# A block-diagonal query made by transposed copies, and state loads moved to the sync engine, in a two-branch transformer kernel

## The chip, the core and the metric

The kernel runs on one core of a Trainium2 chip. A core has a matrix engine (PE, with its weight loads shown as PEld), a vector engine (DVE), a scalar engine (ACT), GpSimd (POOL) and a sync engine (SP). SP, ACT and POOL can start transfers between the core's memory (SBUF) and the chip's memory; matrix products land in PSUM, which DVE and ACT read. The metric is the device time of one execution in microseconds (us).

## The reference

Two inputs go through the same two-layer network: a prompt of 1024 tokens with no past, and eight running sequences of 16 tokens each, with a past. Layer A mixes tokens with an mLSTM recurrence, layer B with attention; each is followed by a feed-forward block. The change lies in layer A's recurrence alone. Cut to what matters:

```
# c: state [heads=8, 128 values, 64 keys], n: normaliser [8, 64], per sequence
def mlstm_chunk(state, q, k, v, log_gates):          # one chunk of tokens
    weights  = exp(gate_a[key] + gate_b[query])      # masked, causal
    num      = (q k^T * weights) v + decay_q * (q c^T)
    den      = row sums of the same, with n for c
    h        = num / max(|den|, floor)
    c_new    = decay * c + (w k)^T v
    n_new    = decay * n + sum(w k)
    return c_new, n_new, h
```

For the prompt the state starts at zero and is carried through eight chunks of 128 tokens. The eight running sequences together are one tile of 128 rows, 16 rows each, and each has an old state of its own: `state_c` is 8 x 8 x 128 x 64 floats (2 MB), `state_n` 8 x 8 x 64.

## The kernel before

Stages follow one another with a barrier of all engines between them. In A1 the first projection is made. In A2 `mlstm` is run twice: for the prompt (tag `mprompt`) and then for the running sequences (`mrun`). A3 holds layer A's output projection, its feed-forward block and layer B's projections, B1 attention, B2 the rest. Each engine carries out its own instructions in the order in which they are written, and a wait on a semaphore holds all that stands behind it on that engine. There is no planner: the order is the order of the code.

**The prompt.** Each chunk has four units, one for a pair of heads. `turn` (L1365) transposes the next chunk's query, key and weighted query on PE, one part in each of units 1 to 3; ACT copies them out of PSUM (L1474). `scores` (L1376) makes the products of key and query, DVE's `argument` (L1544) and ACT's `exponent` (L1469) the weights, DVE's `weighted_scores` (L1553) their product. `numerator` (L1403, L1411) and the state's increment (L1419) follow on PE, and DVE updates the state (L1587). ACT copies the numerators out (L1504). SP loads each chunk's `qk`, `bb` and `v1` (L1265, L1269, L1273) into one of two slots: for the third chunk on, `qk` waits for `k8_done` two chunks back, `bb` for the arguments, `v1` for the numerators. At the end of the first chunk ACT issues the loads of the old running states, 13 transfers (`load_running_states`, L1476 to L1483): four of `nload`, one of `nold`, and eight of `cold`, 256 KB each in runs of 256 bytes.

**The running tile.** PE first transposes the old states, head by head, through one PSUM bank `pt` (L1345); ACT copies each into `c0t` (L1463), and the next head waits for that copy. Then it transposes query and key (L1365). For the old states' part of the numerator, every row of the tile may meet only its own sequence's state. DVE spreads a head's weighted query over all eight sequences and multiplies by a 0/1 matrix (`masked_q`, L1537), PE transposes the result (L1394) into the same bank, ACT copies it (L1500), and PE multiplies by the turned state (L1399). This is done for each of the eight heads, inside `numerator`. At the end DVE makes the output (L1558 to L1563), decays and adds the normaliser (L1606, L1608), and for each head decays the old state (L1612) and adds PE's increment (L1615, from L1456, whose right side `km` POOL makes at L1335). SP stores each head's state (L1286).

The wait that binds the state turns to one another, and the one in front of each query turn:

```
if h: pe.wait_ge(c0_copied, h)                 # L1343: the one bank is free again
pe.wait_ge(qm_done, h + 1)                     # L1390: DVE's masked query
if h >= 1: pe.wait_ge(qm_copied, h)            # L1392: the one bank again
pe.wait_ge(qm_copied, h + 1)                   # L1397: the turned query
```

Of the kernel before, what the change touches and what calls it, by code (L numbers as in the profile page):

```python
# [11 lines left out]
P = 128  # L12
# [7 lines left out]
CB = 512  # L20
# [1171 lines left out]
def mlstm(nc, g, qkvo, b_d, h_d, running, c_out, n_out, state_c=None, state_n=None):  # L1192
    tag = "mrun" if running else "mprompt"
    N_C = 1 if running else NP
    V1 = A_V + 1
    NPAIR = DEC_BATCH // 2
    with Scope(nc, tag) as s:
        SLOTS = 1 if running else 2
        qk, v1 = s.sb("qk", [P, SLOTS, 2 * A_H * A_QK]), s.sb("v1", [P, SLOTS, A_H, V1])
        qg, k8, wsv = s.sb("qg", [P, SLOTS, A_H * A_QK]), s.sb("k8", [P, SLOTS, A_H * A_QK]), s.sb("wsv", [P, SLOTS, A_H, V1])  # L1200
        qt, kt, qgt = (s.sb(n, [P, SLOTS, A_PAIRS, P]) for n in ("qt", "kt", "qgt"))
        tokc, gcc = s.sb("tokc", [P, SLOTS, 4, A_H]), s.sb("gcc", [P, SLOTS, A_PAIRS])
        arg, st = s.sb("arg", [P, A_PAIRS, 2, P]), s.sb("st", [P, 2, 2, P])
        num = s.sb("num", [P, SLOTS, A_H, V1])
        den, hout = s.sb("den", [P, A_H]), s.sb("hout", [P, A_H, A_V])
        bb = s.sb("bb", [P, SLOTS, A_H, P])
        names = ("ones", "tok_done", "qg_done", "k8_done", "wsv_done", "turned", "t_copied",
                 "arg_done", "exp_done", "score_ready", "st_done", "num_ready", "num_done",
                 "state_ready", "state_done", "h_done", "stored", "chain")
        (ones, tok_done, qg_done, k8_done, wsv_done, turned, t_copied,  # L1210
         arg_done, exp_done, score_ready, st_done, num_ready, num_done,
         state_ready, state_done, h_done, stored, chain_sem) = (s.sem(n) for n in names)
        qk_loaded, v_loaded, b_loaded = ([s.sem(f"{n}{i}") for i in range(SLOTS)] for n in ("qk_loaded", "v_loaded", "b_loaded"))

        psc, pn = s.ps("scores", [P, 2, CB]), s.ps("num_p", [P, 2, CB])
        pc, pt = s.ps("state", [P, CB]), s.ps("turn", [P, 4, P])
        final_t, final_c, final_s, made = (s.sem(n) for n in ("final_t", "final_c", "final_s", "made"))
        LINKS = 4
        PARTS = 2 if running else 3
        if running:  # L1220
            cold, nload, nold, c0t = g.cold, g.nload, g.nold, s.sb("c0t", [P, NPAIR, A_H, V1])
            c_loaded, n_loaded = g.c_loaded, g.n_loaded
            qm, km = s.sb("qm", [P, 2, DEC_BATCH, A_QK]), s.sb("km", [P, 2, DEC_BATCH, A_QK])
            qmt, wsk, ccur = s.sb("qmt", [P, 2, NPAIR, P]), s.sb("wsk", [P, A_H, A_QK]), s.sb("ccur", [P, 2, DEC_BATCH, A_QK])
            c0_turned, c0_copied, qm_done, qm_turned, qm_copied = (s.sem(n) for n in (
                "c0_turned", "c0_copied", "qm_done", "qm_turned", "qm_copied"))
            decayed, km_done, wsk_done, c_ready, c_done, n_ready, n_done = (s.sem(n) for n in (
                "decayed", "km_done", "wsk_done", "c_ready", "c_done", "n_ready", "n_done"))
            mask = g.mask_dec
        else:  # L1230
            ct = s.sb("ct", [P, A_PAIRS, V1])
            cfin, nfin = s.sb("cfin", [P, A_PAIRS, P]), s.sb("nfin", [A_PAIRS, P])
            mask = g.mask_kq

        def tile(i):
            return NT - 1 if running else i

        def chunks(engine, body, chain=None):

            if running:  # L1240
                body(0, 0)
            else:
                run(engine, N_C // SLOTS, lambda i: [body(SLOTS * i + slot, slot) for slot in range(SLOTS)],
                    chain, peel_last=True, per=SLOTS * LINKS)
# [4 lines left out]
        def ahead(i, slot, j, n):  # L1249

            return (i, slot, j + n) if j + n < A_PAIRS else (i + 1, 1 - slot, j + n - A_PAIRS)

        def loads(i, slot):

            return (i - slot) * 8 + 16 if SLOTS == 2 else 16

        with nc.Block() as block:

            @block.sync
            def _(sp):  # L1260
                def load(i, slot):
# [6 lines left out]
                    cols = b_d[:, bass.ds(i * P, P)].rearrange("(o h) n -> o h n", o=1)  # L1268
# [4 lines left out]
                    sp.dma_start(v1[:, slot, :, 0:A_V], qkvo[t, :, A_V0:A_O0].rearrange("t (h v) -> t h v", v=A_V)).then_inc(v_loaded[slot], 16)  # L1273

                chunks(sp, load)
                if not running:
                    wait(sp, final_c, 5)
                    for j in range(A_PAIRS):
                        sp.dma_start(c_out[0, 0, 2 * j:2 * j + 2].rearrange("h v d -> v h d"),
                                     cfin[:, j, :].rearrange("v (h d) -> v h d", h=2)).then_inc(final_s, 16)  # L1280
# [335 lines left out]

# [975 lines left out]
```

## Time and profile before

| | us |
|---|---|
| median of three runs | 3476.12 (3471.89 to 3477.49) |
| the profiled execution | 3474.42 |
| its span, first to last instruction | 3472.9 |
| stages ahead of the recurrence | 0 to 348.50 |
| prompt recurrence | 348.50 to 507.95 (159.45; mean granted PE clock 0.61) |
| running recurrence | 507.95 to 572.87 (64.92; mean granted PE clock 0.76) |
| the rest | 572.87 to the end (PE busy 891.90 of 927.13 up to 1500, 1832.13 of 1972.90 after) |

Over the whole span PE is busy for 92%, DVE for 35%, POOL for 34% and ACT for 17%. The granted clock is the share of PE's full speed that it was given: 0.50 is 1.2 GHz, 1.00 is 2.4 GHz. A busy share is an average over the whole kernel; in the two recurrence stages PE waits for short chains of other engines, and these stages have to be read by themselves.

### The profile page before, as it was taken

The page shows a single profiled execution, that of the slowest core. Times are in us where ns is not written, and L with a number is a line of the kernel's source. Part 1 is how long each engine was busy: PE and PEld are TensorE (multiplying, and loading weights), DVE is VectorE, ACT ScalarE, POOL GpSimd, SP SyncE. Part 2 cuts the span into 40 slices and gives each one's busy share as a digit, 9 for nine tenths or more (in the row PEclk, how much of TensorE's full clock was granted, in tenths as well). Part 3 has the DMA queues.
Part 4 walks back from the last instruction along what each step waited for, and adds up shares of the span by engine and source line. Part 5 has one row for each costly group of instructions (what it writes and reads, how often), then busy time and mean ns, then how long its engine had stood idle before and what let it go on. Part 6 is the DMA issues. An engine that isn't in the chain of part 4 may idle for free. (4 is left out here: it accounts for less than half of the span.)

```text
span 3472.9 us, 43103 instructions
## 1 busy us (share of the span) xinstructions
PE 3205.3 (92%) x17102; PEld 2753.7 (79%) x17102; DVE 1220.6 (35%) x1957; ACT 601.7 (17%) x1211; POOL 1196.8 (34%) x682
## 2 busy tenths in 40 slices
PE   7999674999999999989999959997699999999999
PEld 6787453799999999977888846665479999999998
DVE  3110345633332323346235055542344333322323
ACT  3111222220000000012121124443212000000000
POOL 4330214623233433223242136661152322333320
PEclk9999657999999999999999969999899999999999
DMA  4321633311111111111222142326541111111111
GB/s 137 102 86 49 137 104 115 122 37 37 36 36 48 49 48 36 42 38 63 83 91 83 61 108 74 82 61 247 192 163 37 37 36 36 36 60 48 37 36 55
DMA packets 186788, 259.18 MB, mean 75 GB/s; under 512 B 34292, under 2 KB 124248, under 8 KB 186664
## 3 DMA queue, kind: packets, MB, share of 16 engines
q1 hardware_dynamic: 146072, 187.94, 17.8%
q10 hardware_dynamic: 38672, 64.27, 5.3%
q0 software_dynamic: 1920, 5.24, 0.4%
q8 instruction: 86, 1.41, 0.2%
q14 instruction: 38, 0.31, 0.0%
HBM read 198.95 MB, written 50.48 MB: 72 GB/s over the span
## 5 line engine op out<-in xcount | busy, mean ns | idle before, releaser
L858 PE MATMUL A_bank<-A_xth,A_w 128*128 128x384 f32 x1056 | 353.0, 334 | 0.0
L858 PE MATMUL B_bank<-B_xth,B_w 128*128 128x384 f32 x1056 | 353.0, 334 | 0.0
L860 PE MATMUL B_bank<-B_xtl,B_w 128*128 128x384 f32 x1056 | 352.9, 334 | 0.0
L860 PE MATMUL A_bank<-A_xtl,A_w 128*128 128x384 f32 x1056 | 352.9, 334 | 0.0
L859 PE MATMUL A_bank<-A_xth,A_w 128*128 128x384 f32 x1056 | 352.8, 334 | 0.0
L859 PE MATMUL B_bank<-B_xth,B_w 128*128 128x384 f32 x1056 | 352.8, 334 | 0.0
L61 POOL TENSOR_TENSOR A_w1h<-A_raw_a,g_one 128x1024 fp32r<-128x1024 f32 (+1 forms) x43 | 103.0, 2395 | 552.6 <-PE A_bank L886 323.4
L642 PE MATMUL A_bank<-A_w1h,A_xth 128*128 128x512 f32 x576 | 225.4, 391 | 0.0
L644 PE MATMUL A_bank<-A_w1h,A_xtl 128*128 128x512 f32 x576 | 224.3, 389 | 0.0
L643 PE MATMUL A_bank<-A_w1l,A_xth 128*128 128x512 f32 x576 | 224.1, 389 | 0.0
L958 DVE TENSOR_TENSOR g_x<-B_bank,g_x 128x512 f32<-128x512 f32 x198 | 137.0, 692 | 211.3 <-PE B_bank L886 211.3
L958 DVE TENSOR_TENSOR g_x<-A_bank,g_x 128x512 f32<-128x512 f32 x198 | 136.2, 691 | 202.1 <-PE A_bank L886 202.1
L858 PEld LDWEIGHTS A_bank<-A_xth,A_w 128*128 128x128 f32 x1056 | 198.3, 188 | 0.6 <-issue 0.2
L858 PEld LDWEIGHTS B_bank<-B_xth,B_w 128*128 128x128 f32 x1056 | 198.2, 188 | 0.6 <-issue 0.2
L859 PEld LDWEIGHTS A_bank<-A_xth,A_w 128*128 128x128 f32 x1056 | 198.3, 188 | 0.4
L859 PEld LDWEIGHTS B_bank<-B_xth,B_w 128*128 128x128 f32 x1056 | 198.2, 188 | 0.4
L860 PEld LDWEIGHTS A_bank<-A_xtl,A_w 128*128 128x128 f32 x1056 | 198.3, 188 | 0.0
L860 PEld LDWEIGHTS B_bank<-B_xtl,B_w 128*128 128x128 f32 x1056 | 198.2, 188 | 0.0
L1889 POOL TENSOR_TENSOR fprompt_acc<-fprompt_acc,fprompt_prob 128x512 f32<-128x512 f32 (+3 forms) x160 | 152.6, 954 | 60.2 <-ACT fprompt_prob L2075 44.1
L61 POOL TENSOR_TENSOR B_w1h<-B_raw_a,g_one 128x2048 fp32r<-128x2048 f32 (+1 forms) x15 | 47.2, 3148 | 360.6 <-PE B_bank L886 323.4
L884 PE MATMUL A_bank<-A_w1h,A_w1l 128*128 128x512 f32 x396 | 156.8, 396 | 12.1 <-issue 7.3
L61 POOL TENSOR_TENSOR A_w<-A_raw_a,g_one 128x1024 fp32r<-128x1024 f32 x42 | 85.4, 2032 | 238.1 <-PE A_bank L860 64.4
(444 smaller groups left out, 6603.6 us busy)
## 6 DMA issues: line engine op xcount, KB each, us to landing
frun_v<-in_cache_v_dram SPq DMA_DIRECT2D x8, 2048.0 KB, 8.9
qkvo<-A_wide ACTq DMA_DIRECT2D x54, 256.0 KB, 2.0
A_raw_a<-in_w_in_a_dram SPq DMA_DIRECT2D x24, 512.0 KB, 3.7
A_raw_b<-in_w_gu_dram SPq DMA_DIRECT2D x11, 1024.0 KB
A_raw_a<-in_w_down_dram SPq DMA_DIRECT2D x11, 1024.0 KB, 4.9
B_raw_b<-in_w_gu_dram SPq DMA_DIRECT2D x11, 1024.0 KB
B_raw_a<-in_w_down_dram SPq DMA_DIRECT2D x11, 1024.0 KB, 4.9
A_raw_a<-in_w_gu_dram SPq DMA_DIRECT2D x10, 1024.0 KB
```

The lines of the kernel that those rows point to most:

```text
L61: return pool.tensor_tensor(out, in_, ones, ALU.mult)
L642: pe.matmul(bank[:, :], self.mem.xth[:, k, xs], self.wh[par][:, k], start=(k == 0), stop=False)
L643: pe.matmul(bank[:, :], self.mem.xth[:, k, xs], self.wl[par][:, k], start=False, stop=False)
L644: ins = pe.matmul(bank[:, :], self.mem.xtl[:, k, xs], self.wh[par][:, k], start=False, stop=(k == KC - 1))
L858: pe.matmul(banks[j][:, :], h[:, f, k], xth[:, k, self.thirds[j]], start=(k == 0), stop=False)
L859: pe.matmul(banks[j][:, :], l[:, f, k], xth[:, k, self.thirds[j]], start=False, stop=False)
L860: ins = pe.matmul(banks[j][:, :], h[:, f, k], xtl[:, k, self.thirds[j]], start=False, stop=(k == KC - 1))
L884: pe.matmul(self.yp[c][:, :], self.hh[:, f, ts], self.dh[:, f, cs], start=(f == 0), stop=False)
L958: dve.tensor_tensor(xs, self.yp[c][:, :], xs, ALU.add).then_inc(self.added, 1)
L1889: pool.tensor_tensor(to, to, new, ALU.add).then_inc(summed, 1)
```

## The change

`mlstm` becomes two functions. `mlstm_prompt` is the prompt's branch as it was, but for the loads of the old running states: SP issues them, right behind its loads of the second chunk.

```diff
 def load(i, slot):                               # on SP, in mlstm_prompt
     ...
     sp.dma_start(v1[:, slot, :, 0:A_V], ...).then_inc(v_loaded[slot], 16)
+    if isinstance(i, int) and i == 1:
+        load_running_states()
+def load_running_states():                       # on SP
+    for h in range(A_H):
+        sp.dma_start(g.cold[:, h], ...).then_inc(g.c_loaded, 16)
+    for j in range(NPAIR):
+        sp.dma_start(g.nload[j * A_H:(j + 1) * A_H, :], ...).then_inc(g.n_loaded, 16)
+    sp.dma_start(g.nold[:, :], ...).then_inc(g.nold_loaded, 16)
-        if j == A_PAIRS - 1 and not running and below(i, 1):    # on ACT
-            load_running_states()
```

`mlstm_running` is written anew for the one tile. Its core is below. Between the lines shown, POOL makes `k8`, `wsv`, `wsk` and `km` as before; PE transposes `nload` and makes `scores(1)`; DVE waits for the turned query and the zeroes before `place_q`, which runs four times, makes `weighted_scores(0)` before the decays, and after the weights it decays the normaliser, makes the output and adds the normaliser's sum. ACT copies the three turned parts, takes `exponent(0)` and `exponent(1)`, copies the eight turned states and the normaliser's part, takes the last two exponents and copies the numerators. SP loads `qk`, `bb` and `v1`, and stores the output, the normaliser and each head's state as they are done.

```diff
+STEP = P + 2 * DEC_SEQ
+qm = s.sb("qm", [P, A_H, NPAIR * STEP])          # all eight heads at once
+pt = [s.ps(f"turn{i}", [P, 4, P]) for i in range(2)]      # two banks for turns
+pool.memset(v1[:, :, A_V:V1], 1.0).then_inc(ones, 1)
+pool.memset(qm[:, :, :], 0.0).then_inc(zeroed, 1)
+pool.wait_ge(qk_loaded, 16)
+pool.tensor_tensor(qg, qk[:, 0:A_K0], spread(tok[:, KIND_G, :], A_QK), ALU.mult).then_inc(qg_done, 1)
...
+pe.wait_ge(qk_loaded, 16)
+turn(0, qk[:, 0:A_K0]); turn(1, qk[:, A_K0:A_V0])
+pe.wait_ge(qg_done, 1)
+turn(2, qg)                                      # n >= 2 waits for t_copied n - 1
+pe.wait_ge(t_copied, 2)
+scores(0)
+pe.wait_ge(g.c_loaded, 16 * A_H)
+for h in range(A_H):
+    turn_state(h)                                # bank (h + 1) % 2, h >= 2 waits for c0_copied h - 1
...
+pe.wait_ge(qm_done, 4)
+pe.wait_ge(c0_copied, A_H + 1)
+for j in range(A_PAIRS):
+    numerator(j)
+    if j + 2 < A_PAIRS: scores(j + 2)
+def numerator(j):
+    ...
+    for e in range(2):
+        h = 2 * j + e
+        pe.matmul(pn[:, e, 0:V1], st[:, j % 2, e, :], v1[:, h, :], start=True, stop=False)
+        for n in range(NPAIR):
+            ins = pe.matmul(pn[:, e, 0:V1], qm[:, h, n * P:(n + 1) * P], c0t[:, n, h, :], start=False, stop=(n == NPAIR - 1))
+def place_q(e, half):                            # four copies of 64 x 256, into the zeroed buffer
+    rows = slice(half * A_QK, (half + 1) * A_QK)
+    to = qm[rows, :, :].rearrange("p (j e) (n w) -> p j e n w", e=2, w=STEP)[:, :, e, :, half * DEC_SEQ:(half + 1) * DEC_SEQ]
+    got = qgt[e * A_QK:(e + 1) * A_QK, :, :].rearrange("p j (n s t) -> p j n s t", s=2, t=DEC_SEQ)[:, :, :, half, :]
+    dve.tensor_copy(to, got).then_inc(qm_done, 1)
+def decay(h):
+    dve.wait_ge(c0_turned, h + 1)
+    dve.tensor_tensor(cold[:, h], cold[:, h], spread(g.gc_dec[:, h, :], A_QK), ALU.mult).then_inc(decayed, 1)
+for j in range(A_PAIRS): argument(j)
...
+for h in range(A_H): decay(h)
+for j in range(1, A_PAIRS): weighted_scores(j)
...
+for h in range(A_H):
+    dve.wait_ge(c_ready, h + 1)
+    dve.tensor_tensor(cv, late_bank(h), cv, ALU.add).then_inc(c_done, 1)
```

On PE, at the start of the running tile, the order before is this (`mrun_turn` is the one bank for turns, `A_cold` the old states, `mrun_qm` the masked query):

```order
L1345 MATMUL mrun_turn<-g_ident,A_cold 128x128 x32
L1349 MATMUL mrun_turn<-g_ident,A_nload 128x32
L1365 MATMUL mrun_turn<-g_ident,mrun_qk 128x128 x8
L1376 MATMUL mrun_scores<-mrun_qt,mrun_kt 128x128 x4
L1394 MATMUL mrun_turn<-g_ident,mrun_qm 128x128 x4
L1396 MATMUL mrun_num_p<-mrun_v,mrun_st 128x129
L1399 MATMUL mrun_num_p<-mrun_c0t,mrun_qmt 128x129 x4
```

And this is the order now, on the same engine at the same place:

```order
L1545 MATMUL mrun_turn<-g_ident,mrun_qk 128x128 x8
L1545 MATMUL mrun_turn<-g_ident,mrun_qg 128x128 x4
L1562 MATMUL mrun_scores<-mrun_qt,mrun_kt 128x128 x2
L1554 MATMUL mrun_turn<-g_ident,A_cold 128x128 x32
L1588 MATMUL mrun_turn<-g_ident,A_nload 128x32
L1562 MATMUL mrun_scores<-mrun_qt,mrun_kt 128x128 x2
L1571 MATMUL mrun_num_p<-mrun_v,mrun_st 128x129
L1573 MATMUL mrun_num_p<-mrun_c0t,mrun_qm 128x129 x4
```

The turns of query and key have moved ahead of those of the states, the weighted query is turned once (four transposes), and the 32 transposes of the masked query are gone from between the numerators.

On DVE, the end of the running tile before (from the output's last step to the first head's state):

```order
L1560 RECIPROCAL mrun_den<-mrun_den 128x8
L1563 TENSOR_TENSOR mrun_hout<-mrun_num,mrun_den 128x1024
L1606 TENSOR_TENSOR A_nold<-A_nold,A_gc_s 8x512
L1608 TENSOR_TENSOR A_nold<-mrun_state,A_nold 8x512
L1612 TENSOR_TENSOR A_cold<-A_cold,A_gc_dec 128x512
L1615 TENSOR_TENSOR A_cold<-mrun_turn,A_cold 128x512
```

And DVE's running tile now, from its first instruction to the first head's state:

```order
L1642 SCALAR_TENSOR_TENSOR mrun_arg<-mrun_bb,A_tok,A_mask_dec 128x128 x8
L1657 COPY mrun_qm<-mrun_qgt 64x4x4x16 x4
L1650 TENSOR_TENSOR mrun_st<-mrun_scores,mrun_arg 128x256
L1661 TENSOR_TENSOR A_cold<-A_cold,A_gc_dec 128x512 x8
L1650 TENSOR_TENSOR mrun_st<-mrun_scores,mrun_arg 128x256 x3
L1678 TENSOR_TENSOR A_nold<-A_nold,A_gc_s 8x512
...
L1683 TENSOR_TENSOR mrun_hout<-mrun_num,mrun_den 128x1024
L1685 TENSOR_TENSOR A_nold<-mrun_state,A_nold 8x512
L1690 TENSOR_TENSOR A_cold<-mrun_turn,A_cold 128x512
```

All eight decays, and the normaliser's, have moved from the end to the time of the turns; eight masked queries have become four copies.

On SP, in the prompt, this is the order now, from the second chunk's loads to the third chunk's (which were next to one another before):

```order
L1250 DMA mprompt_qk<-qkvo 128x1024
L1254 DMA mprompt_bb<-mlstm_cum_prompt 128x8x128
L1257 DMA mprompt_v<-qkvo 128x8x128
L1240 DMA A_cold<-in_state_c_dram 128x8x64 x8
L1242 DMA A_nload<-in_state_n_dram 8x2x64 x4
L1244 DMA A_nold<-in_state_n_dram 8x512
L95 UNCONDITIONAL_BRANCH
L48 ISA
L1250 ISA
L1250 DMA mprompt_qk<-qkvo 128x1024
```

The third chunk's `qk`, and all that SP loads after it, now stands behind the 13 transfers.

## Rows read from the trace of the kernel before

**Rows 1.** Timeline of ACT at 377 us: start, duration, engine, line, [idle before <- releaser]
```profile
378.97 15.12 ACTq L1483 DMA_DIRECT2D A_cold<-in_state_c_dram  x8
394.14 0.42 ACT L1469 ACTIVATE mprompt_arg<-mprompt_arg 128x256 f32<-128x256 f32 x1 [16.74 <-issue]
```

**Rows 2.** Timeline of PE, 378 to 396 us
```profile
379.12 0.66 PE L1365 MATMUL mprompt_turn<-g_ident,mprompt_qk 128*128 128x128 f32 x4
...
394.97 1.20 PE L1403 MATMUL mprompt_num_p<-mprompt_v,mprompt_st 128*128 128x129 f32 x4 [14.77 <-ACT mprompt_num L1504]
```

**Rows 3.** Timeline of SP in the prompt recurrence
```profile
355.92 3.29 SPq L1273 DMA_DIRECT2D mprompt_v<-qkvo  x1
...
437.51 0.37 SPq L1273 DMA_DIRECT2D mprompt_v<-qkvo  x1
...
453.48 0.37 SPq L1273 DMA_DIRECT2D mprompt_v<-qkvo  x1
...
465.99 0.37 SPq L1273 DMA_DIRECT2D mprompt_v<-qkvo  x1
```

**Rows 4.** The tile `A_cold`: its loads' issue (ns min/median/max), and issue to landing
```profile
L1483 ACTq DMA_DIRECT2D A_cold<-in_state_c_dram x8: 404/1098/5032, 379.0 to 393.2; - x8
...
DMA to landing us min/median/max: 4.5/7.0/10.7
```

**Rows 5.** The tile `mprompt_qk`: issue to landing of its eight loads
```profile
DMA to landing us min/median/max: 3.7/5.8/11.9
```

**Rows 6.** Timeline of PE in the running recurrence
```profile
509.85 1.09 PE L1345 MATMUL mrun_turn<-g_ident,A_cold 128*128 128x128 f32 x4 [0.78 <-ACT mrun_c0t L1463]
511.72 1.09 PE L1345 MATMUL mrun_turn<-g_ident,A_cold 128*128 128x128 f32 x4 [0.78 <-ACT mrun_c0t L1463]
...
523.46 1.12 PE L1365 MATMUL mrun_turn<-g_ident,mrun_qk 128*128 128x128 f32 x4 [0.32 <-ACT mrun_c0t L1465]
...
552.39 1.02 PE L1446 MATMUL mrun_state<-mrun_wsk,A_own 128*8 128x512 f32 x2
```

**Rows 7.** Timeline of POOL in the running recurrence
```profile
511.74 1.04 POOL L1306 TENSOR_TENSOR mrun_qg<-mrun_qk,mrun_tokc 128x512 f32<-128x512 f32 x1 [3.69 <-DMA mrun_qk<-qkvo]
...
560.57 5.39 POOL L1335 TENSOR_TENSOR mrun_km<-mrun_k,A_own 128x512 f32<-128x512 f32 x4 [0.67 <-PE mrun_turn L1456]
```

**Rows 8.** Groups by line, POOL: the largest memset (busy us, mean ns, idle before)
```profile
L1896 POOL MEMSET fprompt_qx<- 128x4096 f32 x1 | 3.7, 3657 | 0.0
```

**Rows 9.** Timeline of ACT at 527 us
```profile
526.98 0.71 ACT L1469 ACTIVATE mrun_arg<-mrun_arg 128x256 f32<-128x256 f32 x2
```

**Rows 10.** Timeline of PE's weight loads, 530 to 537 us
```profile
531.15 1.79 PEld L1399 LDWEIGHTS mrun_num_p<-mrun_c0t,mrun_qmt 128*128 128x128 f32 x8 [0.56 <-ACT mrun_qmt L1500]
...
534.52 0.97 PEld L1399 LDWEIGHTS mrun_num_p<-mrun_c0t,mrun_qmt 128*128 128x128 f32 x8 [0.65 <-ACT mrun_qmt L1500]
...
536.44 0.42 PEld L1394 LDWEIGHTS mrun_turn<-g_ident,mrun_qm 128*128 128x128 f32 x4 [0.53 <-issue]
```

**Rows 11.** Windows: us, busy (instructions) by engine, granted clock, DMA share, GB/s
```profile
508.00:533.00 25.00, 16.13 (x63) 11.43 (x64) 5.48 (x12) 7.84 (x15) 7.43 (x7) 0.50 0.20 64
534.00:552.00 18.00, 13.10 (x99) 11.16 (x99) 4.71 (x9) 5.52 (x11) 0.00 (x0) 1.00 0.00 1
...
565.00:569.00 4.00, 1.80 (x4) 0.30 (x2) 3.45 (x6) 0.00 (x0) 0.96 (x1) 1.00 0.86 178
```

**Rows 12.** Timeline of DVE at 430 us, in the prompt
```profile
430.70 2.46 DVE L1544 SCALAR_TENSOR_TENSOR mprompt_arg<-mprompt_bb,mprompt_tokc,g_mask_kq 128x128 f32<-128x128 f32 x2
...
433.93 0.61 DVE L1544 SCALAR_TENSOR_TENSOR mprompt_arg<-mprompt_bb,mprompt_tokc,g_mask_kq 128x128 f32<-128x128 f32 x2
```

**Rows 13.** Groups by line, DVE, 507 to 573 us
```profile
L1612 DVE TENSOR_TENSOR A_cold<-A_cold,A_gc_dec 128x512 f32<-128x512 f32 x8 | 6.3, 794 | 0.0
...
L1606 DVE TENSOR_TENSOR A_nold<-A_nold,A_gc_s 8x512 f32<-8x512 f32 x1 | 1.5, 1522 | 0.0
```

**Rows 14.** Timeline of DVE, the last instruction of the running recurrence
```profile
567.87 0.69 DVE L1615 TENSOR_TENSOR A_cold<-mrun_state,A_cold 128x512 f32<-128x512 f32 x1
```

More of the change, by code:

```diff
@@ L1213, in mlstm @@
[L1213 to L1217, printed above, removed]
-        LINKS = 4
[L1219 to L1233, printed above, removed]
@@ new lines, in mlstm_prompt @@
+        qk_loaded, v_loaded, b_loaded = ([s.sem(f'{n}{i}') for i in range(SLOTS)] for n in ('qk_loaded', 'v_loaded', 'b_loaded'))
+        psc, pn = (s.ps('scores', [P, 2, CB]), s.ps('num_p', [P, 2, CB]))
+        pc, pt = (s.ps('state', [P, CB]), s.ps('turn', [P, 4, P]))
+        final_t, final_c, final_s, made = (s.sem(n) for n in ('final_t', 'final_c', 'final_s', 'made'))
+        LINKS = 4
+        PARTS = 3
+        ct = s.sb('ct', [P, A_PAIRS, V1])
+        cfin, nfin = (s.sb('cfin', [P, A_PAIRS, P]), s.sb('nfin', [A_PAIRS, P]))
@@ L1235, in tile @@
+        mask = g.mask_kq
         def tile(i):
-            return NT - 1 if running else i
+            return i
         def chunks(engine, body, chain=None):
[L1240 to L1244, printed above, removed]
+            run(engine, N_C // SLOTS, lambda i: [body(SLOTS * i + slot, slot) for slot in range(SLOTS)], chain, peel_last=True, per=SLOTS * LINKS)
@@ L1496, in chunk @@
                             exponent(ni, nj)
-                        if running:
-                            for e in range(2):
-                                act.wait_ge(qm_turned, 2 * j + e + 1)
-                                act.activation(qmt[:, e], pt[:, :, :], ACT.Copy).then_inc(qm_copied, 1)
                         act.wait_ge(num_ready, u + 1)
-                        if j == 0 and not below(i, SLOTS):
+                        if j == 0 and (not below(i, SLOTS)):
                             act.wait_ge(h_done, i - SLOTS + 1)
@@ L1516, in _ @@
                 act.wait_ge(stored, 16 * N_C)
-                if not running:
-                    act.wait_ge(final_t, 1)
-                    for j in range(A_PAIRS):
-                        act.activation(cfin[:, j, :], pt[:, j, :], ACT.Copy).then_inc(final_c, 1)
-                    act.wait_ge(final_t, 2)
-                    act.activation(nfin[:, :], pt[0:A_PAIRS, 0, :], ACT.Copy).then_inc(final_c, 1)
+                act.wait_ge(final_t, 1)
+                for j in range(A_PAIRS):
+                    act.activation(cfin[:, j, :], pt[:, j, :], ACT.Copy).then_inc(final_c, 1)
+                act.wait_ge(final_t, 2)
+                act.activation(nfin[:, :], pt[0:A_PAIRS, 0, :], ACT.Copy).then_inc(final_c, 1)
             @block.vector
@@ L1596, in _ @@
                 weighted_scores(0, 0, 0)
[L1597 to L1601 removed]
+                chunks(dve, chunk, c)
                 finish(N_C - 1, (N_C - 1) % SLOTS)
[L1603 to L1615 removed]
```

374 lines of the change are left out of this document (214 added, 160 removed).

## The prediction

> **What bounds the kernel now.** I read the stages first, as in the table on time and profile: outside the two recurrences PE is busy nearly throughout, and the change touches nothing there. In the two recurrences PE is granted 0.61 and 0.76 of its clock and waits for others, so the argument is about these 224 us alone. Next I read what ACT does when it issues the loads of the old states. The reader is to see that it is caught: it issues eight loads for 15.12 us and starts its next exponent after 16.74 us without work [rows 1]. In that time PE's next matmul waits 14.77 us, for ACT's copy [rows 2]. So these loads cost the prompt about 15 us, not in data that is late but in an engine that is held. Last I read PE's timeline of the running tile: the turns of the old states start every 1.87 us although one takes 1.09, because the one bank is handed to ACT and back [rows 6], and inside the numerators a head's weight loads start 0.56 to 0.65 us after an idle wait for ACT's copy of the masked query [rows 10].
>
> **The loads on SP.** What goes is the wait of 14.8 us [rows 2]. What comes is a wait on SP. SP's second chunk was issued by 355.92 + 3.29 = 359.2 [rows 3]. The same 13 issues there take between 8 x 0.404 = 3.2 us (the shortest issue of `cold`, [rows 4]) and the 16.74 us that ACT lost [rows 1]; I take 16.7, since SP finds its own second chunk still queued, as its issue of 3.29 us instead of 0.37 shows [rows 3]. SP is then free at 376.0. Queued behind are the third chunk's `qk`, `bb` and `v1`; only `qk` has a user soon. It lands 5.8 us after its issue, between 3.7 and 11.9 [rows 5], so at 381.8, and PE wants it for the third chunk's first turn at 379.12 [rows 2]. A new wait of 2.7 us, with ends of 0 and 387.9 - 379.1 = 8.8. The gain is 14.8 - 2.7 = 12.1 us (6.0 to 14.8). ACT's own queue is freed, but nobody was waiting for its transfers.
>
> The Trainium skill speaks against this gain: "DMA: Bandwidth & Descriptors", section "Issuing engines are not separate DMA queues", says that starting transfers from another engine saves only the issuing engine's time, and that this time is usually small beside the transfer. The rows disagree with the second half: the median issue is 1.1 us and the longest 5.0 [rows 4]. By the rule as it stands only the 3.2 us of unhindered issues would be won; that is a rival below.
>
> **The prompt's later chunks.** They are not edited, but their speed hangs on the granted clock. SP's `v1` issue marks the end of a chunk: 453.48 - 437.51 = 15.97 us for one, 465.99 - 453.48 = 12.51 for the next [rows 3]. Without the long idle of PE another chunk or two may run at the short length, or one more at the long. I take nothing, with 3.5 us lost and 6.9 won as ends.
>
> **The running tile up to the numerators.** Before, PE started at once, with states already there. Now it starts with `qk`, which lands 3.7 us in [rows 7]. POOL first zeroes 128 x 5120 elements; the trace has 128 x 4096 at 3.66 us [rows 8], so 4.6, and the weighted query, 1.04 [rows 7], is ready at 5.6, the zeroes costing 0.9. Its turn and copy are one period of 1.87 [rows 6], to 7.5; the first two exponents stand on ACT before the states' copies, 0.71 [rows 9], to 8.2. The eight turns now have two banks, so two heads to a period: 4 x 1.87 = 7.5, to 15.7, and the normaliser's part 0.5 (523.46 less eight periods from 507.98, [rows 6]), to 16.2. Query and key, formerly after the states, are done by then. The numerators start at 16.2. The four copies of the query and the eight decays lie on DVE beside the turns. I price a copy (64 x 256) at no more than the 0.35 of an exponent pass over 256 columns [rows 9], 1.4 together, and the decays at 8 x 0.79 = 6.3 [rows 13]: from about 5 us on, with eight arguments of 0.3 [rows 12], DVE is done at about 15, and the second pair's weights, the first that stand behind the decays, are wanted only after the first pair's numerators. If DVE were later than that, each us would count fully.
>
> **The numerators.** A pair is now ten matmuls of two passes, 20 weight loads. At half clock eight loads take 1.79 us, at full clock 0.97 [rows 10]: 4.5 and 2.4 us a pair. The next pair waits for ACT's copy, 0.95 us from one pair's last load to the next's first (535.49 to 536.44, [rows 10]). Before, the clock was half up to 533, with PE busy for 16 of 25 us, and full from 534 on [rows 11]. I let it rise at the same distance from the start of the stage: two pairs of 5.4 and two of 3.4, less the last gap, 16.7 us. The numerators end at 32.9 us in, at 540.9, where the sum over tokens starts at 552.39 before [rows 6]: 11.5 us won, 15.6 if all four pairs run at full clock, 7.6 if none does.
>
> Against this stands contention. In the prompt, two of DVE's arguments take 2.46 us beside POOL's multiply and 0.61 without it [rows 12]: 1.85 us for one meeting. In the new order DVE's arguments run while POOL works through its list, and ACT's second exponent, ahead of all state copies, needs the first four of them. I take one such meeting, 1.9 us, with none and two (3.7) as ends. The gain is 9.6 us (3.9 to 15.6).
>
> The Trainium skill, "SBUF — State Buffer", section "Who interferes with whom", gives the cause: a vector instruction with two inputs in SBUF and a GpSimd instruction that reads SBUF exclude each other for a whole instruction. The trace agrees, with the 1.85 us. By that rule the zeroes cost DVE nothing, and every decay beside POOL's work may wait.
>
> **The tail.** Before, from 552.39 to the end of the last sum at 568.56 [rows 6, 14] are 16.2 us, of which 1.5 are the normaliser's decay and 6.3 the eight decays [rows 13]. They leave the tail, but POOL's `km` then paces the heads: four in 5.39, 1.35 each [rows 7], against 0.79 + 0.69 = 1.48 on DVE. So 1.5 + 8 x 0.13 = 2.5 us. The upper end is all of 7.9. The lower is nothing, if the stores pace it: they ran at 178 GB/s with the DMA engines 0.86 busy [rows 11], 1.47 us for each head's 256 KB, and the tile's output, 512 KB, now goes through the same queue ahead of them.
>
> **The sum.** 12.1 + 9.6 + 2.5 = 24.2 us. The profiled execution took 3474.4 (its span 3472.9 and 1.5 around it), so 3450.2; the median lies 1.7 above the profiled one, so 3452.
>
> **The rivals.** (1) The third chunk lands late: `qk` takes its longest, 11.9 us, behind the states. For it speaks that 2 MB in short runs stand ahead of it; against it that it is queued only when the last of them has been taken. The gain of the first part is 6.0 and the time 3458. (2) The issue is cheap anyway, and what held ACT was a full set of DMA engines that would have held PE's data too: 3.2 us instead of 12.1, 3461. Against it: PE's wait is ACT's copy [rows 2]. This is the rule of the first Trainium skill page above. (3) The clock helps: two more prompt chunks at 12.5 us and all numerators at full clock (15.6 less the meeting, 4.1 more), 6.9 + 4.1 = 11 us more, 3441. For it: PE idles less everywhere; against it: in the prompt the clock stayed at half for most of the time. (4) All at their bad ends at once: 6.0 - 3.5 + 3.9 + 0 = 6.4 us won, 3470, no change that can be told: this kernel's runs lie within 0.2%, 7 us. (5) Slower: the sync queue crawls. Every load of `cold` takes the longest issue seen, 5.03 us [rows 4], 40.3 together, so SP is free at 399.5 and `qk` lands at 411.4; PE waits 32.3 us instead of 14.8, and a further chunk runs at the low clock (3.5). With the running tile's 12.1 that is 8.9 us lost, 3485. It decides only if the 13 issues take over 41 us, where ACT's took 16.7.
>
> **How the numbers follow.** The forecast has 0.56, late landing 0.17, the cheap issue 0.04, the clock 0.14, the bad ends 0.05, the crawling queue 0.04. Faster are the first four, 0.91; the same 0.05; slower 0.04. The full span of the terms is 3431 (14.8 + 6.9 + 15.6 + 7.9 won) to 3470. The range of 3438 to 3463 holds the forecast, both late cases and most of the clock's, and leaves out the last two.
>
> **What would show it.** ACT's timeline has no state loads and no idle of 16 us; SP's shows the 13 issues from 359 on, and PE waits for the third chunk's turn by 0 to 9 us. In the running tile the state turns come every 0.9 us, the first numerator starts about 16 us in, and no transposes stand between numerators. The decays lie before the second pair's weights, and the last sums follow one another by about 1.35 us. Wrong would be: SP's issues over 25 us; PE idle in front of the first state's turn for the zeroes by more than a few us; DVE's decays delaying the second pair; a tail as long as before with the stores behind it.

## The result and the profile after

The changed kernel takes 3438.01 us (median of four runs, 3436.61 to 3442.11) against 3476.72 for the kernel before on the same chip (3471.89 to 3477.49): a ratio of 0.9894, interval 0.9876 to 0.9911. That is faster by 38.7 us, where about 24 were forecast; it lies 0.01 us above the lower end of the range of 3438 to 3463, and two of its four runs lie below that end.

Its two recurrences, as windows from the first load of each stage to that of the next (length, busy time and instructions of PE, PEld, DVE, ACT and POOL, granted clock, DMA share, GB/s):

```profile
350.24:498.95 148.71, 122.28 (x613) 83.83 (x613) 67.67 (x176) 40.07 (x94) 37.41 (x31) 0.56 0.50 130
498.95:544.75 45.80, 31.69 (x159) 21.31 (x159) 22.51 (x38) 9.45 (x20) 18.49 (x14) 0.84 0.37 93
```

The prompt went from 159.4 to 148.7 us, the running tile from 64.9 to 45.8. Together 29.9 us are gone there. The spans differ by 35.2; the other 5.3 lie in stages that the change does not touch: 1.7 us lost ahead of the recurrences, 7.1 won behind them (experiment 11 tells how far such stages differ by themselves).

**The loads.** Timeline of SP after, which answers to [rows 1, 3, 4]:

```profile
361.28 15.15 SPq L1240 DMA_DIRECT2D A_cold<-in_state_c_dram  x8
376.47 1.80 SPq L1242 DMA_DIRECT2D A_nload<-in_state_n_dram  x4
378.32 0.30 SPq L1244 DMA_DIRECT2D A_nold<-in_state_n_dram  x1
379.05 0.38 SPq L1250 DMA_DIRECT2D mprompt_qk<-qkvo  x1
```

The eight loads hold SP for 15.15 us, as they held ACT for 15.12. The third chunk's `qk` is issued at 379.05. On PE neither its turn nor the chunk's first numerator, which waited 14.77 us in [rows 2], waits:

```profile
382.47 0.70 PE L1346 MATMUL mprompt_state<-mprompt_wsv,mprompt_k 128*64 128x129 f32 x4
383.10 1.12 PE L1309 MATMUL mprompt_turn<-g_ident,mprompt_qk 128*128 128x128 f32 x4
...
384.88 1.23 PE L1331 MATMUL mprompt_num_p<-mprompt_v,mprompt_st 128*128 128x129 f32 x4
```

No line has idle time in brackets. In [rows 2] the turn took 0.66 us, here 1.12, so PE is at half clock. The stage began 1.7 us later than before (350.24 against 348.51); counted from its start PE reaches the turn at 32.9 us instead of 30.6, 2.3 later than I assumed.

**The running tile.** Timeline of PE after (some rows), to be held against [rows 6, 10]:

```profile
506.39 6.01 PE L1554 MATMUL mrun_turn<-g_ident,A_cold 128*128 128x128 f32 x32
...
513.41 0.46 PE L1571 MATMUL mrun_num_p<-mrun_v,mrun_st 128*128 128x129 f32 x2 [0.39 <-ACT mrun_c0t L1628]
...
517.54 0.49 PE L1562 MATMUL mrun_scores<-mrun_qt,mrun_kt 64*128 64x128 f32 x4 [1.66 <-DVE mrun_st L1650]
...
518.29 1.50 PE L1573 MATMUL mrun_num_p<-mrun_c0t,mrun_qm 128*128 128x129 f32 x8
...
520.02 1.92 PE L1573 MATMUL mrun_num_p<-mrun_c0t,mrun_qm 128*128 128x129 f32 x8
...
527.95 1.02 PE L1599 MATMUL mrun_state<-mrun_wsk,A_own 128*8 128x512 f32 x2
```

All eight states are turned in 6.0 us. The numerators start 14.5 us into the tile, lose 1.66 us to DVE once, and end at 29.0, where it was 44.4 [rows 6]. The windows of the same stretch, to set beside [rows 11]:

```profile
502.00:508.50 6.50, 5.75 (x26) 4.66 (x27) 4.41 (x8) 3.11 (x7) 6.50 (x5) 0.50 0.49 163
508.50:518.50 10.00, 7.73 (x57) 5.92 (x56) 9.23 (x16) 5.18 (x11) 2.59 (x3) 1.00 0.00 0
518.50:522.00 3.50, 3.50 (x20) 3.28 (x18) 0.06 (x1) 0.02 (x1) 0.00 (x0) 0.53 0.00 0
```

The clock is full 9.6 us into the tile instead of 26, and falls once for 3.5 us, right behind the 1.66 us without work. What DVE did there (some rows):

```profile
504.09 5.05 DVE L1642 SCALAR_TENSOR_TENSOR mrun_arg<-mrun_bb,A_tok,A_mask_dec 128x128 f32<-128x128 f32 x8 [13.64 <-DMA mrun_bb<-mlstm_cum_running]
...
509.07 2.82 DVE L1657 COPY mrun_qm<-mrun_qgt 64x256 f32<-64x256 f32 x4
511.92 0.42 DVE L1650 TENSOR_TENSOR mrun_st<-mrun_scores,mrun_arg 128x256 f32<-128x256 f32 x1
512.26 4.90 DVE L1661 TENSOR_TENSOR A_cold<-A_cold,A_gc_dec 128x512 f32<-128x512 f32 x8
517.07 0.42 DVE L1650 TENSOR_TENSOR mrun_st<-mrun_scores,mrun_arg 128x256 f32<-128x256 f32 x1
```

The second pair's weights stand behind eight decays and are late. The eight arguments, 0.3 us each where DVE was undisturbed [rows 12], take 5.05 here, while POOL works through its multiplies; a copy of the query costs 0.70 us on the mean. Two of the last sums, the second answering to [rows 14], and the stores of the states:

```profile
536.96 0.69 DVE L1690 TENSOR_TENSOR A_cold<-mrun_state,A_cold 128x512 f32<-128x512 f32 x1 [0.68 <-PE mrun_state L1607]
...
539.33 0.69 DVE L1690 TENSOR_TENSOR A_cold<-mrun_state,A_cold 128x512 f32<-128x512 f32 x1 [0.68 <-PE mrun_state L1607]
```
```profile
531.63 9.12 SPq L1516 DMA_DIRECT2D out_dram<-A_cold  x8
```

From the sum over tokens to the end of the last sum are 12.07 us, before 16.17. The two sums shown are two heads apart: 2.37 us, 1.19 a head.

### The profile page after: what moved, and what is told of

Its sections match the earlier page's. It is cut to its first block and busy times, and to the rows that moved or that the text cites. A ratio compares the mean times of both kernels' runs of the same rounds, so it can differ in the third digit from the quotient of the medians.

```text
span 3437.7 us, 43009 instructions
## 1 busy us (share of the span) xinstructions
PE 3195.1 (93%) x17074; PEld 2748.6 (80%) x17074; DVE 1220.3 (35%) x1952; ACT 598.3 (17%) x1204; POOL 1202.0 (35%) x683
```

## The experiments

The theory after this reading: ACT was held by its own issuing; the running tile gained by itself, through the order and density of PE's work, and lost some of it to DVE. Lengths of stages are from each run's profiled execution, "rest" is its span less the two recurrences; ratios are against the kernel before, run beside each on its chip (medians of 3471.4 to 3475.1 us in the experiments). The diffs are shown shortened, with `...` or a comment for what is left out.

| | prompt | running | rest | median | ratio (interval) |
|---|---|---|---|---|---|
| before | 159.44 | 64.92 | 3248.5 | 3476.7 | |
| changed | 148.71 | 45.80 | 3243.2 | 3438.0 | 0.9894 (0.9876 to 0.9911) |
| 1 loads on SP only | 148.30 | 65.26 | 3245.9 | 3461.4 | 0.9974 (0.9963 to 0.9984) |
| 2 running tile only | 156.50 | 44.06 | 3237.5 | 3451.3 | 0.9949 (0.9933 to 0.9966) |
| 3 one bank | 150.21 | 50.34 | 3241.8 | 3445.6 | 0.9934 (0.9917 to 0.9950) |
| 4 late decays | 146.75 | 46.05 | 3252.9 | 3446.3 | 0.9913 (0.9900 to 0.9927) |
| 5 weights first | 144.91 | 42.62 | 3238.0 | 3433.5 | 0.9900 (0.9882 to 0.9917) |
| 6 eight key buffers | 148.59 | 45.42 | 3249.4 | 3443.5 | 0.9916 (0.9902 to 0.9930) |
| 7 loads twice | 159.02 | 45.83 | 3240.8 | 3447.0 | 0.9919 (0.9906 to 0.9932) |
| 8 states first | 150.96 | 43.31 | 3242.8 | 3440.0 | 0.9898 (0.9885 to 0.9912) |
| 9 quiet POOL | 148.18 | 42.57 | 3244.3 | 3439.4 | 0.9897 (0.9883 to 0.9912) |
| 10 query by head | 144.25 | 51.56 | 3248.8 | 3448.3 | 0.9922 (0.9908 to 0.9935) |
| 11 changed again | 150.68 | 46.09 | 3246.4 | 3443.7 | 0.9904 (0.9888 to 0.9920) |
| 12 quiet POOL, two keys | 145.33 | 40.00 | 3252.3 | 3435.9 | 0.9883 (0.9863 to 0.9904) |

**1. The loads alone.**

```diff
 # the kernel before; on SP, behind the loads of the second chunk
+if not running and isinstance(i, int) and i == 1: load_running_states()   # dma_start by sp
-if j == A_PAIRS - 1 and not running and below(i, 1): load_running_states() # on ACT
```

> The kernel before, with one edit: the loads of the running states are issued by SP at the place they have in the changed kernel; the running tile's function is the old one. Theory (ACT was held by its own issuing, and the prompt's third chunk with it): the prompt stage shrinks from 159.4 to about 149 us, the running tile stays at 65 us, the time falls by about 11 us against the kernel before. Rival (the issuing itself was cheap, and the chunk waited for something else that stays): the fall is 3 us or less. Second rival (the roughly 7 us that the later stages lost in the profile of the changed kernel hang on this move): the fall is about 18 us.

The prompt took 148.3 us, the running tile 65.3; the runs fell by 9.0 us (0.26% of 3471, interval 5.6 to 12.8). The theory's place and size hold, both rivals are out.

**2. The running tile alone.**

```diff
 # the changed kernel; on ACT, at the end of the prompt's first chunk
+if j == A_PAIRS - 1 and below(i, 1): load_running_states()
-if isinstance(i, int) and i == 1: load_running_states()                   # on SP
```

> The changed kernel, with the loads of the running states back on ACT at their old place: the new running tile alone. Theory (the running tile gains by itself, as its tensor engine work is packed closely enough to get the full clock within some 7 us of the first matmul): the running tile takes about 46 us as in the changed kernel, the prompt about 159 us as before, the time falls by about 19 us against the kernel before. Rival (the clock came early because of what the prompt's shorter third chunk left behind): the clock comes about 25 us into the tile as in the kernel before, the tile takes some 51 to 55 us, the fall is 10 to 14 us.

The prompt took 156.5 us, 2.5 less than the theory had; ACT is held again, as this piece of its timeline shows:

```profile
380.07 15.57 ACTq L1376 DMA_DIRECT2D A_cold<-in_state_c_dram  x8
395.68 0.42 ACT L1363 ACTIVATE mprompt_arg<-mprompt_arg 128x256 f32<-128x256 f32 x1 [17.20 <-issue]
```

The tile took 44.1 us, and the clock was full 7.4 us into it. The early clock is thus the tile's own, and the rival is out by the tile's length; by whole runs alone (11.8 to 23.3 us) it would not be. Here the second pair waited longer than in the changed kernel, and the clock stayed full (PE, and two windows as above):

```profile
524.02 0.49 PE L1562 MATMUL mrun_scores<-mrun_qt,mrun_kt 64*128 64x128 f32 x4 [2.22 <-DVE mrun_st L1650]
```
```profile
520.32:523.32 3.00, 1.47 (x14) 1.28 (x12) 3.00 (x6) 0.39 (x1) 0.00 (x0) 1.00 0.00 0
523.32:526.32 3.00, 2.30 (x20) 2.19 (x21) 1.07 (x3) 0.00 (x0) 0.00 (x0) 1.00 0.00 0
```

The 9.0 and the 17.7 us (0.51%) of the two halves add up to 26.7; by its ratios the whole change won 36.9 and, in experiment 11, 33.4. The intervals are too wide to say whether more than the sum is won.

**3. One bank.**

```diff
-pe.transpose(pt[(h + 1) % 2][:, n, :], cold..., g.ident)      # turn_state, and ACT's copy
+pe.transpose(pt[1][:, n, :], cold..., g.ident)                # h waits for c0_copied h
```

> The changed kernel, with the states turned through one PSUM bank instead of two, so that each group of four turns waits for ACT's copy of the group before. Theory (two banks both shorten the turning and pack the tensor engine, and the packing brings the clock): turning takes about 8 x 1.2 to 1.9 us instead of 6, the numerators start 4 to 9 us later, and the clock is half for a part of them, which adds 2 to 5 us more: the running tile takes 52 to 58 us, the time is 6 to 12 us above the changed kernel. Rival (the early clock does not hang on the turning): the numerators run at full clock as before and the tile is later by the turning alone, 4 us at most, the time within 5 us of the changed kernel.

PE at the start of the turns, in their middle, and at the first numerator:

```profile
507.99 0.66 PE L1554 MATMUL mrun_turn<-g_ident,A_cold 128*128 128x128 f32 x4 [0.69 <-ACT mrun_c0t L1626]
...
513.37 1.11 PE L1554 MATMUL mrun_turn<-g_ident,A_cold 128*128 128x128 f32 x4 [0.69 <-ACT mrun_c0t L1626]
...
519.76 0.80 PE L1571 MATMUL mrun_num_p<-mrun_v,mrun_st 128*128 128x129 f32 x2
```

The clock rose as early as with two banks, while the query was turned and the first states: that part of the theory is wrong. Under the repeated waits of 0.69 us it fell again (1.11 for what took 0.66), and the numerators started 20.6 us in, 6.1 later. The tile took 50.3: 4.4 more than the mean of the changed kernel's two profiles. That is below the theory's 52 to 58 and a little above the rival's 50, and neither stands as put: the rise does not hang on the banks, but the numerators began at half clock. They were 6.1 us later, and a part was given back, since the second pair's weights were no longer late. Whole runs lie about 10 to 14 us above the changed kernel's ratios, nearer the theory's 6 to 12 than the rival's 5, but a spread of several us lies on them (experiment 11).

**4. Decays at their old place.**

```diff
-for h in range(A_H): decay(h)                    # behind weighted_scores(0)
 for h in range(A_H):                             # the last loop
+    decay(h)
     dve.wait_ge(c_ready, h + 1)
```

> The changed kernel, with the decay of the old states put back into the last loop, one head ahead of that head's sum, as in the kernel before. Theory (the early decays are what shortened the tail): the stretch from the first sum of keys to the end of the last head's sum goes back from 12.1 us to about 16, and as the weights of the second pair no longer stand behind decays, 3 to 4 us come back there: the running tile stays at 44 to 47 us. Rival (a decay of 0.61 us hides in DVE's wait for each head's product, so the tail owes nothing to it): the tail stays at 12 to 13 us and the tile falls to about 42 us, as with the weights put first.

In the tail DVE's decays run beside POOL's keys:

```profile
525.38 1.35 DVE L1661 TENSOR_TENSOR A_cold<-A_cold,A_gc_dec 128x512 f32<-128x512 f32 x1
526.77 0.69 DVE L1689 TENSOR_TENSOR A_cold<-mrun_state,A_cold 128x512 f32<-128x512 f32 x1
527.37 0.94 DVE L1661 TENSOR_TENSOR A_cold<-A_cold,A_gc_dec 128x512 f32<-128x512 f32 x1
```

The tail grew to 16.4 us, the sum over tokens came 3.4 earlier; the tile took 46.05, as changed. The theory holds: early decays are worth 4.4 us in the tail, and in the order of the change they cost nearly as much at the numerators.

**5. Weights before the last five decays.**

```diff
-for h in range(A_H): decay(h)
-for j in range(1, A_PAIRS): weighted_scores(j)
+for h in range(3): decay(h)
+weighted_scores(1)
+for h in range(3, A_H): decay(h)
+for j in range(2, A_PAIRS): weighted_scores(j)
```

> The changed kernel, with the weights of the second pair of heads computed after three of the eight decays instead of after all eight. Theory (the second numerator waited 1.66 us for weights that stood behind the decays on DVE, and the idle time cost the clock as well): the wait goes, the stretch at half clock behind it goes, the running tile falls from 45.8 to about 42 us, 3 to 4 us below the changed kernel. Rival (only the wait goes, the clock falls for another reason): the tile falls to about 44 us. Second rival (the decays, now later, hold the last sums): the tile stays at 45 to 46 us.

The second pair follows with no wait, at full clock:

```profile
510.41 0.49 PE L1562 MATMUL mrun_scores<-mrun_qt,mrun_kt 64*128 64x128 f32 x4
511.04 0.46 PE L1571 MATMUL mrun_num_p<-mrun_v,mrun_st 128*128 128x129 f32 x2
511.34 1.06 PE L1573 MATMUL mrun_num_p<-mrun_c0t,mrun_qm 128*128 128x129 f32 x8
```

42.6 us, 3.3 below the changed kernel's mean, as the theory said. That a gap by itself brings the clock down is not shown by it: in experiment 2 the same wait was 2.22 us long, and the clock stayed at 1.00. Against that run's 44.1 the gain is 1.4.

**6. Eight key buffers.**

```diff
 # experiment 5, and
-km = s.sb("km", [P, 2, DEC_BATCH, A_QK])         # h >= 2 waits for c_ready h - 1
+km = s.sb("km", [P, A_H, DEC_BATCH, A_QK])       # no wait
```

> The changed kernel, with the weights of the second pair put after three decays, and the keys of each head kept in a buffer of their own (eight in place of two), so that POOL makes all of them ahead of the tail. Theory (the tail is paced by POOL, which remakes a pair of buffers only when the tensor engine is done with them: 1.04 us each and a hand-over of 0.27): the tail from the first sum of keys shrinks from 12.1 to about 10 us, the running tile from about 42.6 to 40 to 41. Rival (POOL's eight products now lie beside the decays and the numerators and slow DVE): the tail shrinks, but the decays stretch by up to half and the numerators come 1 to 3 us later, so that the tile stays at 42 to 44.

The tail shrank to 10.7 us, but the copies of the query now run into POOL's keys:

```profile
L1655 DVE COPY mrun_qm<-mrun_qgt x4: 1020/1022/1125, 509.0 to 512.3; 64x256 f32<-64x256 f32 x4
```

(Minimum, median and maximum in ns.) PE waited 1.41 us for the weights, the clock fell for 4 us, and the tile took 45.4: the rival, a little worse than it said.

**7. Loads issued twice.**

```diff
+for h in range(A_H):                             # on SP, behind the first eight; nothing reads cold2
+    sp.dma_start(g.cold2[:, h], state_c[:, 0, h]...)
```

> The changed kernel, with the eight loads of the old states issued twice on SP, the second time into a tile of their own that nothing reads. Theory (issuing holds the engine for 1.9 us a load, and the next chunk's query and keys stand behind it on SP, with little to spare): SP is free some 15 us later, the tensor engine waits about 12 to 15 us for the third chunk, the prompt stage grows from 149 to 160 to 164 us. Rival (the third chunk has slack on SP, or issuing goes faster when the queue is not held back): the prompt stage stays within 3 us of 149.

SP's second eight, and the third chunk's first turn on PE:

```profile
375.22 9.45 SPq L1242 DMA_DIRECT2D A_cold<-in_state_c_dram  x8
```
```profile
391.23 1.11 PE L1311 MATMUL mprompt_turn<-g_ident,mprompt_qk 128*128 128x128 f32 x4 [9.44 <-DMA mprompt_qk<-qkvo]
```

9.45 us of issuing became 9.44 of waiting, and the prompt took 159.0: 10.3 of the 10.7 us won were gone. SP has next to no slack at that place; only the size (1.2 us a load instead of 1.9) was below the theory's.

**8. Half of the states turned first.**

```diff
 # experiment 6, and on PE
+for h in range(4): turn_state(h)                 # ahead of the wait for qk
 turn(0, ...); turn(1, ...); turn(2, qg); scores(0)
+for h in range(4, A_H): turn_state(h)
 # on DVE: two pairs of arguments, the four copies, weighted_scores(0), then the other two pairs
```

> As the kernel with eight key buffers, and in the running tile half of the old states are turned while the query and the keys are still being loaded, and DVE places the turned query after two pairs of arguments instead of after four. Theory (the numerators are held by the chain of turns and by DVE's arguments, and the tensor engine's first 8 us without work are the place for the turning): the numerators start 11 to 12 us into the tile instead of 14.5, the tile falls by about 3 us more, to 37 to 38. Rival (the turns then run at half clock and with gaps, and the clock is still half at the numerators): they start 13 us in and take 3 us more, the tile stays at 40 to 42.

PE was ready for the numerators 9.7 us in and then waited 2.96 us for DVE, whose four copies took 5.16 us beside POOL; they started at 13.1, the first pair at half clock behind that wait, and the tile took 43.3. Neither stood as put: the place was free, as the theory has it, but the limit had moved to DVE; the rival's start and half clock came, but its time of 40 to 42 did not.

**9. POOL held back.**

```diff
 # experiment 8, and on POOL ahead of wsv, wsk and km
+pool.wait_ge(arg_done, A_PAIRS)                  # and DVE's last two decays behind all weights
```

> As the kernel that turns half of the states first, but POOL holds its weighted values and keys back until DVE has made all its arguments, so that the four copies of the turned query run alone; two decays come after the last weights. Theory (POOL's multiplies beside DVE's copies stretched these from 2.1 us for the four to 5.2, and that, not the tensor engine, set the start of the numerators): the four copies take about 2.1 us, the numerators start 10 to 11 us into the tile in place of 13.1, the clock has no gap of 3 us to fall in, and the tile takes 37.5 to 39.5 us. Rival (the copies are slow for their stride, whatever POOL does): they stay at 4 us or more, the numerators start 12 us in or later, the tile stays at 41 to 43. Second rival (POOL's held work is late for the tail): the numerators start early, but the sum of keys waits, the tile stays at 40 to 42.

PE's first turns, DVE's copies, and the start of the tail:

```profile
498.21 3.75 PE L1555 MATMUL mrun_turn<-g_ident,A_cold 128*128 128x128 f32 x16 [4.64 <-PEq L122]
```
```profile
L1665 DVE COPY mrun_qm<-mrun_qgt x4: 286/288/292, 506.4 to 507.3; 64x256 f32<-64x256 f32 x4
```
```profile
526.60 1.21 PE L1610 MATMUL mrun_state<-mrun_km,mrun_wsv 128*128 128x512 f32 x2 [2.71 <-DVE A_nold L1698]
```

Alone a copy takes 0.29 us where it took 1.02: the slowness was POOL's doing. The numerators started 12.0 us in, later than the theory's 10 to 11. But POOL's eight keys, 11.6 us, then lay on the decays (4.09 us for the second three) and the tail began with a wait of 2.71: 42.6, the second rival's course at a somewhat higher price than its 40 to 42. The first rival's 41 to 43 holds the number, but its cause, the stride, is out.

**10. Query turned by head.**

```diff
-place_q(e, half)                                 # the zeroes, the third turn and the four copies go
+masked_q(h)                                      # DVE; PE turns it, ACT copies it in each head's numerator
```

> The changed kernel, with one part undone: the weighted query is again masked by DVE for each head, turned by the tensor engine and copied by ACT inside that head's numerator (with two banks in turn), and there are no zeroes and no four copies. Theory (each head's chain of mask, turn and copy stalls the tensor engine, and its gaps cost the clock too): a pair of numerators takes 5 to 6 us instead of 3, the clock is half for much of it, and the tile takes 56 to 62 us, 10 to 16 above the changed kernel. Rival (what was won lies in the turning of the states and in the decays, and the query turned by head costs only its 32 more turns): the tile takes 49 to 51 us.

```profile
510.44 1.16 PE L1580 MATMUL mrun_num_p<-mrun_c0t,mrun_qmt 128*128 128x129 f32 x8 [0.46 <-ACT mrun_qmt L1637]
```

PE waits 0.46 us for ACT in every head, and a pair comes every 5.3 us instead of every 3.0 (experiment 5), as the theory put it. But the clock was full from 11 us into the tile to its end, so that half of the theory is wrong, and the second pair had no stall. The tile took 51.6, 5.6 above the changed kernel's mean, next to the rival's 49 to 51.

**11. The changed kernel again.** No edit.

> The changed kernel once more, unaltered, beside the others on one chip. Theory (the stages that the change does not touch differ from one execution to the next, by the clock that is granted, and the 7 us that the later stages lost in its first profile are such a spread): the recurrences take 146 to 151 and 43 to 46 us again, the other stages together differ by several us from the first profile, the time lies within 8 us of 3438. Rival (the 7 us belong to the change, by what it leaves for later stages): the other stages repeat their first times within 2 us.

The recurrences repeat within 2 us (150.7 and 46.1; the wait for the second weights is 1.82 us), the rest does not: 3246.4 us against 3243.2, and over all profiles 3237.5 to 3252.9, where the kernels are the same. The 5.3 us are within that spread, and the rival is out. So whole times a few us apart settle nothing here; the recurrences' own lengths do, the prompt's to within some 3 us, since it varies between 144.3 and 151.0 in the profiles with the loads once on SP, and the tile's to within 2, since the changed tile took 44.1 to 46.1 in its four profiles (changed, 2, 7 and 11).

**12. POOL held back, two key buffers.**

```diff
 # experiment 9, and
-km = s.sb("km", [P, A_H, DEC_BATCH, A_QK])
+km = s.sb("km", [P, 2, DEC_BATCH, A_QK])         # h >= 2 waits for c_ready h - 1
```

> As the kernel in which POOL waits for DVE's arguments, but with two key buffers again, so that POOL rests from its second key on and the later decays run alone. Theory (in the kernel with eight buffers POOL's 11.6 us of keys lay on DVE's decays and made the sum of the normaliser late, 2.7 us of wait and a stretch at half clock behind it): the numerators start 12 us into the tile, the wait goes back to 1.0 us, the tail takes 12.1 us, and the tile 40 to 41 us, the shortest of all; the whole time falls by about 35 us against the kernel before, within the spread of the stages that are not touched. Rival (the early start is eaten by something else on DVE, since its work is the same): the tile stays at 42 to 43 us.

```profile
350.71:496.04 145.33, 111.63 (x613) 76.81 (x613) 69.77 (x176) 39.65 (x94) 37.46 (x31) 0.63 0.52 133
496.04:536.04 40.00, 30.65 (x159) 20.67 (x159) 21.19 (x38) 9.22 (x20) 19.49 (x14) 0.88 0.43 106
```

40.0 us, the shortest tile, 5.9 below the changed kernel's mean, as the theory said. The whole time is 3435.9 (0.9883, 0.9863 to 0.9904): below the kernel before, but not to be told from the changed kernel by whole runs.

## Why the prediction was right or wrong

**The loads on SP: right, with two terms off that cancel.** The wait of 14.8 us went (experiments 1 and 2). The new wait, put at 2.7, was 0: `qk` was issued at 379.05, but PE, at half clock, reached the turn 2.3 us later in the stage than before. That half clock cost 3.0 us, about what the missing wait gave: by the end of the second chunk 11.8 us were won, at the stage's end 10.7, against the 12.1 of the term. That the two cancel is luck. Experiment 7 shows that the reasoning with the queue was sound, us for us.

The rule of "DMA: Bandwidth & Descriptors" in the Trainium skill, section "Issuing engines are not separate DMA queues", that the issuing engine's time is usually small beside the transfer, did not hold here, with 15.15 us on SP; its other half, that only the issuing engine's time is saved by the move, fits experiment 1.

**The prompt's later chunks: right.** Put at nothing, they lost 1.1 us (11.8 less 10.7).

**The running tile up to the sum over tokens: the step that was mis-sized.** The term was 9.6 us, measured 15.4. Three pieces make up the 5.8. The numerators started 14.5 us in instead of 16.2: 1.7, as the turning took 6.0 and not 7.5. They took 14.5 us instead of 16.7: 2.2. And 1.9 had been set aside for contention. The root of the second is one assumption: "I let it rise at the same distance from the start of the stage". The clock was full 9.6 us in. Experiment 2 shows that this belongs to the new tile and experiment 3 that two banks are not needed for the rise, only for keeping it there: in both the stage opens with twelve turns of query, key and weighted query in one piece, where the kernel before opened with turns that each waited 0.78 us [rows 6]. That query and key come first is not needed: experiments 8, 9 and 12 open with sixteen turns of the states in one piece, ahead of a single wait of 0.78, and the clock is full about 3, 9 and 9 us in. That the opening without waits is the cause is argued, not isolated, since no run brings the waits back there. Undone one at a time, the second bank is worth 4.4 us (experiment 3), the copied query 5.6 (experiment 10) and the early decays nothing on balance (experiment 4); if these prices add, the other 9 of the tile's 19.1 us were not taken apart. Without the stall in the second pair, experiment 5, the term would have been 18.4.

**Contention and the copies: present, but the charge fell in the wrong place.** The meeting set aside for the first exponents did not delay the numerators. The arguments, put at 8 x 0.3 = 2.4 us, took 5.05 beside POOL, where four of them alone take 1.13 (experiment 9); the copies, "no more than 0.35", took 0.70, and are 0.29 alone (experiment 9) and 1.02 beside POOL (experiments 6 and 8). "SBUF — State Buffer", section "Who interferes with whom", in the Trainium skill says of such copies too that they can take the port pair shared with GpSimd and then shut it out, or be shut out, for a whole instruction. The trace agrees: the longer ones are about one instruction of POOL each (1.04 us for a key).

**The decays: the sentence that they lie beside the turns was wrong.** Arguments and copies made DVE late, by 2.6 and 1.4 us, so the decays began only as the turning ended, at 512.26, and the second pair's weights were "wanted" 1.66 us before they came. The prediction named this as what would show it wrong; its price was 3.3 us (experiment 5; 1.4 against experiment 2, where the clock did not fall).

**The tail: right in kind.** 4.1 us instead of 2.5. POOL's keys pace it, as put, but at 1.19 us a head and not 1.35: a key takes 1.04, with a hand-over of 0.27 for every two, and the 1.35 was read from four keys made beside DVE's decays. By the prediction's own sum, 1.5 + 8 x (1.48 - 1.19) = 3.8. The normaliser's decay cost nothing there. A late decay beside POOL costs up to 1.35 us, so that experiment 4 gives back 4.4. The stores did not pace it.

The forecast of 24.2 us stands against 29.9 in the recurrences (27.6 in the second profile), and the rest up to 38.7 lies within the spread of the untouched stages. The third rival, the clock, told the mechanism of the largest piece of the difference: its price for the running tile was 4.1. Its other half, 6.9 us in the prompt, did not come. That 3438.01 still lies in the range is luck: without those 8.8 us the time would be some 9 us higher, well inside it, and with a median 0.02 lower it would be outside.

## What to carry to other kernels

Issuing loads can hold an engine for long (here 15 us for eight), so charge it like compute and look at what stands behind it on that engine; moved to another, it needs slack there. Do not carry a clock profile over from the old order of instructions: bound it by both levels. A vector engine's short copies and decays should not be priced by their time alone while POOL has a list to work through; the shortest tile had a wait that keeps POOL quiet for 4 us, while the buffers that let POOL run ahead cost 2.8 us (experiment 6 against 5) and 2.6 (9 against 12).

## What the runs showed of the hardware that was not expected

- The same eight loads took 15.1 us to issue on ACT and on SP; a second eight behind them on SP took 9.45.
- The clock of PE fell behind waits of 1.66 us (1.82 in the second profile), 1.41 (experiment 6) and 2.96 (experiment 8), but not behind one of 2.22 in experiment 2; it fell under repeated waits of 0.69 (experiment 3) and held through experiment 10 with a wait of 0.46 in every head. What else it hung on stays open.
- A 64 x 256 copy on DVE takes 0.29 us alone, and mostly 1.02 to 1.13 beside POOL (once 2.01, experiment 8).
- With nothing changed, the untouched stages differ by up to 15 us between executions.
